# HGRN2 trunk on eight cores: two small per-chunk products moved to GpSimd, and ring slots given back two groups later

## The chip, the cores and the metric

One Trainium2 chip, all eight cores, one batch element per core; the cores do not talk to each other. The metric is the device time in microseconds of the slowest core. PE is TensorE, ACT ScalarE, DVE VectorE, POOL GpSimd and SP the sync engine.

## The reference, cut to what matters

Four pre-norm layers on a residual x of 2048 positions by 1024 channels. Layers 0 and 2 are an attention layer with a short convolution, layers 1 and 3 are HGRN2, a gated linear recurrence; each is followed by a SwiGLU. The change touches the HGRN2 layers alone. Cut to its core, one of them is, for each of 8 heads of 128 channels:

```python
q, f_logit, v, g_out = split(rms_norm(x) @ w_in, 4)
f = lb + (1 - lb) * sigmoid(f_logit);  k = 1 - f
for each chunk:                      # b = cumsum(log f) inside the chunk
    o     = (q * exp(b)) @ state + (masked, decayed q k^T) @ v
    k_dec = k * exp(b_last - b)      # the decayed keys
    state = exp(b_last)[:, None] * state + k_dec.T @ v
o = o * rsqrt(mean(o*o)) * head_norm * silu(g_out);  x += o @ w_out
```

## The kernel before, in words

Everything is kept transposed, channels on partitions. The residual `xT_sb` (f32) and the normed input `hT_sb` (bf16) stay in SBUF, scratch is one tensor `U`, and the eight PSUM banks are `ps`. Each engine works its instructions off in the order in which they are written; a small tracker adds the semaphore waits. Thus an instruction that waits holds up all that stands behind it on its engine.

**An HGRN2 layer.** `hgrn_layer` works on chunks of 128 positions, 16 to a head, in four quarters q of four chunks. The order is written out by hand as a list of slots: `slot(P, fl)` issues one projection item from a list (8 matmuls of 128x512 for f, g and q, L884, or 16 of 128x256 for v, L933), and then what `at[P]` holds. A head n takes slots P0 = 16n and after: four f items, four g items, four v items (none in the last head, n = 7), four q items. The projection items rotate over PSUM banks 0 to 2. `pump` puts the evacuation of an item behind the matmuls of the next item, so the matmuls of item k can start only when the evacuation of item k-3 is done. The evacuations are on ACT for f (L897, sigmoid), g (L904, silu) and v (L945, copy), and on DVE for q (L914).

**What the slots carry beside the projections.** For head n: slot P0+8 has the logs of f (`prep_ln`, L954, ACT), slots P0+9 and P0+10 the prefix sums of the two halves (`prep_scan`, L961, DVE) and `prep_mid` (L969 to L973, DVE), slots P0+11 and P0+12 the exponentials of the two halves (`prep_exp`, L991 and L992, ACT; `prep_gsc`, L980 to L986, the factors per chunk, in `gsc`). Slots P0+13 to P0+16 have `prep_k` (L997, DVE), the keys of quarter q. For each quarter q, with c0 = P0+4q:

- slot c0+14, `b_ke`: the keys of the quarter times the chunk's factor, 128x512 in bf16, into one buffer `KE0` (L1004, DVE).
- slot c0+16, `b_ta`: PE transposes these (L1018) and makes the scores inside the chunks (L1026, L1028).
- slot c0+17, `b_kd`: DVE copies the transposes out (L1037) and masks the scores (L1039).
- slot c0+18, `b_u`: PE multiplies them with v (L1051).
- slot c0+19, `b_w`: for each chunk DVE adds to the running f32 state (L1067, L1064 for the first), and ACT makes a scaled bf16 copy of it, 128x128, in one of eight buffers `SB` (L1072).
- slot c0+22, `b_pvi`: PE multiplies scores with v (L1082) and the bf16 state with q (L1085); ACT squares the result (L1090). Then `b_og` (L1096), the norm (`b_ss` L1101, `b_norm` L1106 and L1109) and `b_ot` (L1115).

As c0 moves by four, slots of the form 4k+2 hold `b_u` of a quarter, `b_pvi` of the one before and `b_ke` of the next, and slots of the form 4k+3 hold `b_w`. The last head is followed by 22 slots in which the output projection (`OutProj`, L421, with the residual add L426) runs along.

**The weights.** `WStream` streams all weights through `ring`, 19456 bytes a partition, in the order of use. `release` marks a slot free, and `_pump` at once issues the next load that fits; the loads stand in POOL's queue (L268), and each waits there until the matmuls that read the old contents of its place are done. One head needs 10240 bytes of ring: 2048 each for f, g and q, 4096 for v. In an HGRN2 layer POOL does nothing else but these loads and two loads of output weights into `U` (L454). The releases are in `proj_items` and `v_items`, in the slot of the item's last matmuls.

Of the kernel before, what the change touches and what calls it, by code (L numbers as in the profile page):

```python
# [8 lines left out]
AF = mybir.ActivationFunctionType  # L9
ALU = mybir.AluOpType  # L10
# [110 lines left out]
def flat_res(*items):  # L121
    out = []
    for it in items:
        if isinstance(it, Res):
            out.append(it)
        elif isinstance(it, Buf):
            out.extend(it.res)
        else:
            for x in it:
                out.extend(flat_res(x))  # L130
    return out

def build(layers, final, n_ab, n_c, n_ffn, comps=("mix", "ffn")):
    nc = bass.Bass("TRN2", target_bir_lowering=False)
    es = contextlib.ExitStack()
    T = Tracker()
# [23 lines left out]
    with es:  # L160
# [16 lines left out]
        ACT = Eng(nc, es, "act", nc.scalar)  # L177
        DVE = Eng(nc, es, "dve", nc.vector)
        POOL = Eng(nc, es, "pool", nc.gpsimd)
# [27 lines left out]
        def abuf(off, nbytes, dt=BF16, parts=128, shape=None):  # L207
            assert off % 4 == 0 and off + nbytes <= NUNITS * 4096
            ap = Uf[0:parts, off // 2:(off + nbytes) // 2]
            if dt == F32:  # L210
                ap = ap.bitcast(F32)
            if shape is not None:
                ap = ap.rearrange(shape[0], **shape[1])
            return Buf(ap, u_res[off // GRAN:(off + nbytes - 1) // GRAN + 1])
# [13 lines left out]
        class WStream:  # L228
            def __init__(self):
                self.plan = []  # L230
                self.i_issue = 0
                self.i_get = 0
                self.live = []
                self.head = 0
                self.slots = {}

            def _place(self, nbytes):
                nb = -(-nbytes // GRAN) * GRAN
                if not self.live:
                    return 0, nb  # L240
                tail = self.live[0][0]
                if self.head > tail:
                    if self.head + nb <= RING_BYTES:
                        return self.head, nb
                    if nb <= tail:
                        return 0, nb
                    return None
                if self.head + nb <= tail:
                    return self.head, nb
                return None  # L250
# [33 lines left out]
                    self._pump()  # L284
                return self.slots.pop(i)

            def release(self, bf):
                if T.plan:
                    return
                for e in self.live:  # L290
                    if e[2] == bf.widx:
                        e[3] = True
                while self.live and self.live[0][3]:
                    self.live.pop(0)
                self._pump()

        W = WStream()

# [535 lines left out]
        def hgrn_layer(gl, ci, rd, gnext):  # L834
# [7 lines left out]
            def quarter(base, q, n=1, dt=BF16):  # L842
                sz = 1024 if dt == BF16 else 2048
                return abuf(base + q * sz, n * sz, dt)
# [15 lines left out]
            def pump(fl):  # L860
                if fl:
                    mm, evac = fl.pop(0)
                    b = nbank[0] % 3
                    nbank[0] += 1
                    mm(b)
                    pend.append((evac, b))
                    if len(pend) > 1:
                        e, eb = pend.pop(0)
                        e(eb)
# [6 lines left out]
            def proj_items(key, src, h, evac):  # L876
                w = W.get((key, gl, h), src, NKC, 128)
                fl = []
                for q in range(4):
                    def mm(b, q=q):  # L880
                        def fn():
                            inst = None
                            for kc in range(NKC):
                                inst = nc.tensor.matmul(ps[:, b, :], lhsT=w.ap[:, kc, :],  # L884
                                                        rhs=hT[:, kc, q * 512:(q + 1) * 512],
                                                        start=(kc == 0), stop=(kc == NKC - 1))
                            return inst
                        T.op(PE, fn, reads=flat_res(w, h_res), writes=[bank[b]])
                        if q == 3:
                            W.release(w)  # L890
                    fl.append((mm, lambda b, q=q: evac(b, q)))
                return fl

# [25 lines left out]
            def v_items(pair, part, parts):  # L919
                n = 8 // parts  # L920
                w = W.get(("c_v", gl, pair, part), c_v_d[ci, pair], NKC, 256)
                fl = []
                for i in range(n):
                    t2 = part * n + i

                    def mm(b, t2=t2, i=i):
                        def fn():
                            inst = None
                            for k in range(2):
                                o = ps[:, b, :].rearrange("p (a k e) -> p a k e", a=2, k=2)[:, :, k, :]  # L930
                                tt = 2 * t2 + k
                                for kc in range(NKC):
                                    inst = nc.tensor.matmul(o, lhsT=hT[:, kc, tt * 128:(tt + 1) * 128],  # L933
                                                            rhs=w.ap[:, kc, :].rearrange("p (a e) -> p a e", a=2),
                                                            start=(kc == 0), stop=(kc == NKC - 1))
                            return inst
                        T.op(PE, fn, reads=flat_res(w, h_res), writes=[bank[b]])
                        if i == n - 1:
                            W.release(w)

                    def evac(b, t2=t2):
                        o = Uf[:, 2 * pair * 2048:(2 * pair + 2) * 2048].rearrange("p (a x) -> p a x", a=2)[
                            :, :, t2 * 256:(t2 + 1) * 256]
                        res = [r for a in range(2) for r in abuf((2 * pair + a) * 4096 + t2 * 512, 512).res]
                        T.op(ACT, lambda: nc.scalar.copy(out=o, in_=ps[:, b, :].rearrange("p (a x) -> p a x", a=2)),  # L945
                             reads=[bank[b]], writes=res)
                    fl.append((mm, evac))
                return fl
# [52 lines left out]
            def b_ke(h, q):  # L1001
                n = 4 if q < 3 else 3
                kt, ke = KT(q), quarter(KE0, 0)
                T.op(DVE, lambda: nc.vector.tensor_tensor(  # L1004
                    out=ke.ap[:, 0:n * 128].rearrange("p (a c) -> p a c", a=n),
                    in0=kt.ap[:, 0:n * 128].rearrange("p (a c) -> p a c", a=n),
                    in1=gsc[:, h % 2, 0, 4 * q:4 * q + n].rearrange("p (c o) -> p c o", o=1).broadcast_to([128, n, 128]),
                    op=ALU.mult),
                    reads=flat_res(kt, gsc_res[h % 2]), writes=ke.res)
# [46 lines left out]
            def b_w(h, q):  # L1056
                n = 4 if q < 3 else 3
                for i in range(n):
                    c = 4 * q + i
                    u = ps[:, 6, i * 128:(i + 1) * 128]  # L1060
                    sn, sp = Wb[c % 4], Wb[(c - 1) % 4]
                    gr = gsc_res[h % 2]
                    if c == 0:
                        T.op(DVE, lambda: nc.vector.tensor_copy(out=sn.ap, in_=u), reads=[bank[6]], writes=sn.res)  # L1064
                    else:
                        b12 = gsc[:, h % 2, 2, c - 1:c]
                        T.op(DVE, lambda: nc.vector.scalar_tensor_tensor(out=sn.ap, in0=sp.ap, scalar=b12, in1=u,  # L1067
                                                                         op0=ALU.mult, op1=ALU.add),
                             reads=flat_res(sp, gr, bank[6]), writes=sn.res)
                    b1 = gsc[:, h % 2, 1, c:c + 1]  # L1070
                    sbn = SB[(c + 1) % 8]
                    T.op(ACT, lambda: nc.scalar.activation(out=sbn.ap, in_=sn.ap, func=AF.Copy, scale=b1),  # L1072
                         reads=flat_res(sn, gr), writes=sbn.res)

            def b_pvi(h, q):
# [81 lines left out]
                    at[P0 + 13 + q].insert(0, (prep_k, (q,))) if P0 + 13 + q in at else put(P0 + 13 + q, prep_k, q)  # L1157

            def slot(P, fl):
                if fl:  # L1160
                    pump(fl)
                for fn, args in at.get(P, []):
                    fn(*args)
# [10 lines left out]
            for k in range(8):  # L1174
                slot(4 + k, v)
# [180 lines left out]
```

How the kernel before makes its waits and increments, by code:

```python
    def _wait(self, eng, reads, writes):  # L82
        deps = {}
        for r in reads:
            self._merge(deps, r.writers)
        for w in writes:
            self._merge(deps, w.writers)
            self._merge(deps, w.readers)
        for so, v in deps.items():
            if so is eng and eng.skip_self:
                continue
            if eng.waited.get(so, 0) >= v:
                continue
            eng.h.wait_ge(so.sem, v)
            eng.waited[so] = v
# [1 line left out]
    def op(self, eng, fn, reads=(), writes=()):  # L97
# [3 lines left out]
        inst = fn()  # L101
        eng.cnt += 1
        inst.then_inc(eng.sem, 1)
        for r in reads:
# [1136 lines left out]
        def body():  # L1241
            stages = []
            for (gl, mi, fi) in layers:
                if "mix" in comps:
                    stages.append((hgrn_layer if gl % 2 else fox_layer, gl, mi, C_GMIX + gl * 8))
                if "ffn" in comps:
                    stages.append((ffn, gl, fi, C_GFFN + gl * 8))
            gnext = [s[3] for s in stages[1:]] + [C_GFIN if final else None]
            rd = first_norm(stages[0][3])
            for k, ((fn, gl, i, _), gn) in enumerate(zip(stages, gnext)):
                rd = fn(gl, i, rd, gn)
                if k == 0:
                    T.dma(POOL, sem_cst, lambda: nc.gpsimd.dma_start(out=cst[:, K_SCAN:NCONST], in_=const_d[:, K_SCAN:NCONST]),
                          writes=[scan_res])
            rd.need(3)
            if not T.plan:
                nc.sync.wait_ge(sem_out.sem, sem_out.cnt)
```

## Time and profile before

| | us |
|---|---|
| median of 3 runs | 3595.34 |
| the three runs | 3595.34, 3595.16, 3924.01 |
| the profiled execution, its own time | 3592.3 |
| its span, slowest core (core 5) | 3591.3 |
| spans of all cores | 3582.7 to 3591.3 |

Busy share of core 5: PE 93%, DVE 40%, ACT 36%, POOL 4%. The two HGRN2 layers take about 925 to 1330 us and 2770 to 3180 us of the span. In a row of a timeline the first number is the start and the second the length in us; xN says how many instructions the row merges; what stands in brackets is the idle time of the engine before it and what ended it. "PEclk" is the clock granted to TensorE, 1.00 being 2.4 GHz and 0.50 being 1.2 GHz; in a stretch where it changed it is the mean.

### The profile page before, as it was taken

The page shows a single profiled execution, that of the slowest core. Times are in us where ns is not written, and L with a number is a line of the kernel's source. Part 1 is how long each engine was busy: PE and PEld are TensorE (multiplying, and loading weights), DVE is VectorE, ACT ScalarE, POOL GpSimd, SP SyncE. Part 2 cuts the span into 40 slices and gives each one's busy share as a digit, 9 for nine tenths or more (in the row PEclk, how much of TensorE's full clock was granted, in tenths as well). Part 3 has the DMA queues.
Part 4 walks back from the last instruction along what each step waited for, and adds up shares of the span by engine and source line. Part 5 has one row for each costly group of instructions (what it writes and reads, how often), then busy time and mean ns, then how long its engine had stood idle before and what let it go on. Part 6 is the DMA issues. An engine that isn't in the chain of part 4 may idle for free.

```text
span 3591.3 us, 47292 instructions; the slowest of 8 cores (3582.7 to 3591.3 us)
## 1 busy us (share of the span) xinstructions
PE 3344.1 (93%) x17264; PEld 1604.9 (45%) x17264; DVE 1447.6 (40%) x2159; ACT 1290.8 (36%) x2067; POOL 156.2 (4%) x256
## 2 busy tenths in 40 slices
PE   6999999999888889999989898999998888899998
PEld 2444344444454434444445443444444554344443
DVE  6443521113467672111374445111145667611215
ACT  3666511002477741101236564110135776411013
POOL 1000000000000000000020000000000000000000
PEclk9999999999999999999999999999999999999999
DMA  5111132121122113112100110312201221131212
GB/s 130 22 19 24 18 62 40 31 47 27 19 33 36 19 30 59 34 31 47 24 15 13 31 30 13 64 28 43 42 15 30 36 33 30 18 64 33 38 30 94
DMA packets 42289, 131.00 MB, mean 36 GB/s; under 512 B 4448, under 2 KB 4704, under 8 KB 42048
## 3 DMA queue, kind: packets, MB, share of 16 engines
q0 software_dynamic: 33120, 110.54, 17.9%
q1 hardware_dynamic: 8944, 17.44, 1.5%
q8 instruction: 144, 2.36, 0.3%
q14 instruction: 81, 0.66, 0.1%
HBM read 229.90 MB, written 8.59 MB: 66 GB/s over the span
## 4 chain that ended last, share of the span: by engine, by line
PE 86%; ACT 5%; DVE 4%; issue 3%; DMA 1%; ACTq 0%; DVEq 0%; SPq 0%; POOLq 0%; POOL 0%
PE ps L304 32%; PE ps L421 11%; PE ps L507 11%; PE ps L314 10%; PE ps L884 9%; PE ps L817 4%; PE ps L754 3%; PE ps L342 2%; PE ps L646 2%; PE ps L933 2%; DVE hT_sb L360 1%; DVE xT_sb L426 1%; ACT U L799 1%; DVE U L1067 1%; ACT U L954 1%
## 5 line engine op out<-in xcount | busy, mean ns | idle before, releaser
L304 PE MATMUL ps<-hT_sb,ring 128*128 128x512 bf16 x5248 | 1134.0, 379 | 6.7 <-ACT U L484 6.7
L304 PEld LDWEIGHTS ps<-hT_sb,ring 128*128 128x128 bf16 x5248 | 513.2, 98 | 626.8 <-issue 8.5
L484 ACT ACTIVATE U<-ps 128x2048 bf16<-128x2048 f32 x88 | 165.2, 1877 | 1371.4 <-PE ps L304 1371.3
L487 DVE TENSOR_TENSOR U<-U,ps 128x2048 bf16<-128x2048 bf16 x84 | 192.1, 2287 | 950.2 <-PE ps L304 923.0
L884 PE MATMUL ps<-hT_sb,ring 128*128 128x512 bf16 x1536 | 377.1, 399 | 74.4 <-ACT U L945 45.8
L314 PE MATMUL ps<-hT_sb,ring 128*128 128x512 bf16 (+1 forms) x1728 | 410.0, 385 | 25.2 <-DVE U L624 11.1
L507 PE MATMUL ps<-U,ring 128*128 128x512 bf16 x1792 | 387.4, 379 | 0.0
L799 ACT ACTIVATE U<-ps 128x512 bf16<-128x512 f32 (+3 forms) x640 | 303.3, 536 | 208.5 <-PE ps L758 122.1
L421 PE MATMUL ps<-U 128*128 128x512 bf16 x1536 | 372.5, 383 | 3.8 <-DMA U<-c_out 2.6
L426 DVE TENSOR_TENSOR xT_sb<-xT_sb,ps 128x512 f32<-128x512 f32 x320 | 218.4, 686 | 206.3 <-PE ps L421 187.2
L332 ACT ACTIVATE U<-xT_sb 128x512 bf16<-128x512 f32 x288 | 177.7, 628 | 287.1 <-DVE xT_sb L426 274.7
L507 PEld LDWEIGHTS ps<-U,ring 128*128 128x128 bf16 x1792 | 175.3, 98 | 211.5
L314 PEld LDWEIGHTS ps<-hT_sb,ring 128*128 128x128 bf16 (+1 forms) x1728 | 166.0, 98 | 228.3 <-issue 44.8
L884 PEld LDWEIGHTS ps<-hT_sb,ring 128*128 128x128 bf16 x1536 | 152.7, 102 | 257.0 <-issue 110.4
L817 PE MATMUL ps<-U 128*128 128x512 bf16 (+3 forms) x640 | 219.6, 347 | 34.2 <-ACT U L799 32.9
L421 PEld LDWEIGHTS ps<-U 128*128 128x128 bf16 x1536 | 150.2, 98 | 182.2 <-issue 8.1
L754 PE MATMUL ps<-U 70*128 70x512 bf16 (+3 forms) x640 | 220.7, 349 | 0.0
L512 DVE TENSOR_TENSOR xT_sb<-xT_sb,ps 128x2048 f32<-128x2048 f32 x32 | 73.2, 2287 | 313.6 <-PE ps L507 313.6
L360 DVE SCALAR_TENSOR_TENSOR hT_sb<-xT_sb,small_sb,U 128x512 bf16<-128x512 f32 x256 | 183.6, 746 | 37.4 <-ACT U L348 34.3
L342 PE MATMUL ps<-U,cst_sb 128*128 128x512 bf16 x288 | 115.4, 411 | 52.5 <-ACT U L332 36.6
L933 PE MATMUL ps<-ring,hT_sb 128*128 128x256 bf16 x1024 | 119.0, 273 | 20.4 <-ACT U L945 20.4
L1072 ACT ACTIVATE U<-U,gsc 128x128 bf16<-128x128 f32 x240 | 95.9, 402 | 113.2 <-DVE U L1067 91.5
(113 smaller groups left out, 2522.9 us busy)
## 6 DMA issues: line engine op xcount, KB each, us to landing
ring<-ffn_in POOLq DMA_DIRECT2D x88, 512.0 KB, 5.3
ring<-ffn_out POOLq DMA_DIRECT2D x16, 896.0 KB, 7.1
xT_sb<-xT SPq DMA_DIRECT2D x8, 1024.0 KB, 19.5
U<-ffn_out POOLq DMA_DIRECT2D x16, 512.0 KB, 12.1
yT<-xT_sb SPq DMA_DIRECT2D x16, 512.0 KB, 2.9
ring<-c_v POOLq DMA_DIRECT2D x14, 512.0 KB, 5.3
ring<-ab_qk POOLq DMA_DIRECT2D x8, 512.0 KB, 6.4
ring<-ab_cx POOLq DMA_DIRECT2D x8, 512.0 KB, 6.5
```

The source lines that it names most:

```text
L304: inst = nc.tensor.matmul(ps[0:m, banks[tt], :], lhsT=w.ap[:, kc, c0:c0 + m], rhs=hT[:, kc, tt * 512:(tt + 1) * 512], start=(kc == 0), sto ...
L314: inst = nc.tensor.matmul(ps[0:m, b, :], lhsT=w.ap[:, kc, c0:c0 + m], rhs=hT[:, kc, t * 512:(t + 1) * 512], start=(kc == 0), stop=(kc == N ...
L360: T.op(DVE, lambda: nc.vector.scalar_tensor_tensor(out=dst[:, c, sl], in0=xT[:, c, sl], scalar=small[:, self.gcol + c:self.gcol + c + 1], ...
L421: inst = nc.tensor.matmul(ps[:, b, :], lhsT=w.ap[:, self.jmap[j], cs], rhs=rr[j - j0].ap, start=(j == ja), stop=(j == jb - 1))
L426: T.op(DVE, lambda: nc.vector.tensor_tensor(out=xT[:, dc, sl], in0=xT[:, dc, sl], in1=ps[:, b, :], op=ALU.add), reads=[bank[b], x_res[dc][ ...
L487: T.op(DVE, lambda: nc.vector.tensor_tensor(out=v4(ubuf(jj, 1).ap), in0=v4(st.ap), in1=ps[:, 4:8, :], op=ALU.mult), reads=flat_res(st, ban ...
L507: inst = nc.tensor.matmul(ps[:, b0 + tt, :], lhsT=wo.ap[:, j, dcl * 128:(dcl + 1) * 128], rhs=a.ap[:, tt * 512:(tt + 1) * 512], start=(j = ...
L754: inst = nc.tensor.matmul(ps[:, sbk, off:512], lhsT=k_.ap[0:70, j * 128:(j + 1) * 128], rhs=q_.ap[0:70, qt * 512 + off:(qt + 1) * 512], st ...
L799: T.op(ACT, lambda: nc.scalar.activation(out=pt.ap[:, off:512], in_=ps[:, sbk, off:512], func=AF.Exp), reads=[bank[sbk]], writes=pt.res)
L817: T.op(PE, lambda: nc.tensor.matmul(ps[:, ob, off:512], lhsT=v.ap[:, j, vs], rhs=pt.ap[:, off:512], start=(j == 0), stop=(j == 4 * qt + 3) ...
L884: inst = nc.tensor.matmul(ps[:, b, :], lhsT=w.ap[:, kc, :], rhs=hT[:, kc, q * 512:(q + 1) * 512], start=(kc == 0), stop=(kc == NKC - 1))
L933: inst = nc.tensor.matmul(o, lhsT=hT[:, kc, tt * 128:(tt + 1) * 128], rhs=w.ap[:, kc, :].rearrange("p (a e) -> p a e", a=2), start=(kc == ...
```

## The change

It does three things.

- `b_ke` issues its product on POOL in place of DVE.
- In `b_w` the bf16 copy of the state is a `tensor_scalar` on POOL in place of an `activation` on ACT.
- In `proj_items` and `v_items` the ring slot is not released at once. It is put on a list with a count of two. `tick`, called at the start of every slot of an HGRN2 layer, counts down, and releases what has come to zero: the next load of the ring is issued at the start of the second slot after the one with the item's last matmuls.

```diff
+            def release(self, bf, late=False):
                 if T.plan:
+                    return
+                if late:
+                    self.late.append([2, bf])
                     return
...
+            def tick(self):
+                for e in self.late:
+                    e[0] -= 1
+                while self.late and self.late[0][0] <= 0:
+                    self.release(self.late.pop(0)[1])
...
                         if q == 3:
-                            W.release(w)
+                            W.release(w, True)
...
                         if i == n - 1:
-                            W.release(w)
+                            W.release(w, True)
...
                 kt, ke = KT(q), quarter(KE0, 0)
-                T.op(DVE, lambda: nc.vector.tensor_tensor(
+                T.op(POOL, lambda: nc.gpsimd.tensor_tensor(
...
                     sbn = SB[(c + 1) % 8]
-                    T.op(ACT, lambda: nc.scalar.activation(out=sbn.ap, in_=sn.ap, func=AF.Copy, scale=b1),
+                    T.op(POOL, lambda: nc.gpsimd.tensor_scalar(out=sbn.ap, in0=sn.ap, scalar1=b1, scalar2=None, op0=ALU.mult),
...
             def slot(P, fl):
+                W.tick()
                 if fl:
                     pump(fl)
```

ACT before, in slots P0+8 to P0+12 of a middle head. L954 is the logs, L945 the evacuations of v, L1106 and L1109 the norm, L1090 the square, L1072 the state copies, L991 and L992 the exponentials of the first half:

```order
L954 ACTIVATE U<-U,deriv_sb 128x1024 x2
L945 CAST U<-ps 128x2x256 x2
L1106 ACTIVATE U<-ps,deriv_sb 128x512
L1109 ACTIVATE U<-U 128x512
L1090 ACTIVATE U<-ps 128x512
L945 CAST U<-ps 128x2x256
L1072 ACTIVATE U<-U,gsc 128x128 x4
L991 ACTIVATE U<-U 128x1024
L992 ACTIVATE U<-U 128x1024
L945 CAST U<-ps 128x2x256
```

The same place of the changed kernel, where the lines stand 10 lower in the file (L955 is the old L945, L1001 the old L991):

```order
L964 ACTIVATE U<-U,deriv_sb 128x1024 x2
L955 CAST U<-ps 128x2x256 x2
L1116 ACTIVATE U<-ps,deriv_sb 128x512
L1119 ACTIVATE U<-U 128x512
L1100 ACTIVATE U<-ps 128x512
L955 CAST U<-ps 128x2x256
L1001 ACTIVATE U<-U 128x1024
L1002 ACTIVATE U<-U 128x1024
L955 CAST U<-ps 128x2x256
```

Four copies no longer stand between the third evacuation of v and the exponentials, behind which the fourth evacuation of v stands; all else keeps its order.

POOL before, over a little more than one middle head, is loads alone:

```order
L268 DMA ring<-c_g 128x1024
L268 DMA ring<-c_v 128x2048
L268 DMA ring<-c_q 128x1024
L268 DMA ring<-c_f 128x1024
L268 DMA ring<-c_g 128x1024
```

POOL of the changed kernel over one middle head (L1014 is `b_ke`, L1082 the state copies, L269 a ring load):

```order
L1014 TENSOR_TENSOR U<-U,gsc 128x512
L1082 TENSOR_SCALAR U<-U,gsc 128x128 x4
L269 DMA ring<-c_q 128x1024
L1014 TENSOR_TENSOR U<-U,gsc 128x512
L1082 TENSOR_SCALAR U<-U,gsc 128x128 x4
L269 DMA ring<-c_f 128x1024
L1014 TENSOR_TENSOR U<-U,gsc 128x384
L1082 TENSOR_SCALAR U<-U,gsc 128x128 x4
L269 DMA ring<-c_g 128x1024
L1014 TENSOR_TENSOR U<-U,gsc 128x512
L1082 TENSOR_SCALAR U<-U,gsc 128x128 x3
```

Each group of copies (slot 4k+3) is followed by the ring load that was given back late (slot 4k+5), and then by the next quarter's decayed keys (slot 4k+6).

## Rows read from the trace of the kernel before

**Rows 1.** The page, busy time, share of span, instructions of each engine.

```profile
PE 3344.1 (93%) x17264; PEld 1604.9 (45%) x17264; DVE 1447.6 (40%) x2159; ACT 1290.8 (36%) x2067; POOL 156.2 (4%) x256
```

**Rows 2.** Waits of PE, 925 to 1330: total us, times, longest.

```profile
PE ps L884 <- ACT U L945: 23.1, 6, 4.1
PE ps L933 <- ACT U L945: 10.1, 9, 1.5
...
PE ps L884 <- ACT U L904: 5.8, 1, 5.8
```

**Rows 3.** Waits of PE, 2770 to 3180.

```profile
PE ps L884 <- ACT U L945: 22.7, 6, 3.8
```

**Rows 4.** Busy time by stretch, one middle head from one long wait to the next.

```profile
core 5: us, PE busy (x) PEld busy (x) DVE busy (x) ACT busy (x) POOL busy (x), PEclk, DMA share, GB/s
...
1044.87:1085.56 40.69, 35.75 (x258) 21.15 (x259) 28.20 (x54) 29.61 (x50) 2.11 (x4) 0.96 0.21 33
```

**Rows 5.** Timeline of PE, 1044 to 1090.

```profile
1065.74 1.89 PE L884 MATMUL ps<-hT_sb,ring 128*128 128x512 bf16 x8
...
1075.58 1.91 PE L933 MATMUL ps<-ring,hT_sb 128*128 128x256 bf16 x16 [1.15 <-ACT U L945]
...
1085.56 2.83 PE L884 MATMUL ps<-hT_sb,ring 128*128 128x512 bf16 x8 [3.79 <-ACT U L945]
1088.18 0.53 PE L1051 MATMUL ps<-U 128*128 128x128 bf16 x3
```

**Rows 6.** Timeline of ACT, 1044 to 1090.

```profile
1067.80 1.70 ACT L1072 ACTIVATE U<-U,gsc 128x128 bf16<-128x128 f32 x4 [0.71 <-DVE U L1067]
1069.40 0.58 ACT L904 ACTIVATE U<-ps 128x512 bf16<-128x512 f32 x1
...
1072.61 2.36 ACT L954 ACTIVATE U<-U,deriv_sb 128x1024 f32<-128x1024 f32 x2
...
1077.61 0.58 ACT L945 CAST U<-ps 128x512 bf16<-128x512 f32 x1
1081.09 1.76 ACT L1072 ACTIVATE U<-U,gsc 128x128 bf16<-128x128 f32 x4 [2.90 <-DVE U L1067]
1082.75 1.04 ACT L991 ACTIVATE U<-U 128x1024 f32<-128x1024 f32 x1
...
1084.85 0.57 ACT L945 CAST U<-ps 128x512 bf16<-128x512 f32 x1
```

**Rows 7.** Timeline of DVE, 1044 to 1090.

```profile
1073.94 2.29 DVE L961 TENSOR_TENSOR_SCAN U<-cst_sb,U 128x1024 f32<-128x1024 bf16 x1 [0.38 <-ACT U L954]
1076.14 0.53 DVE L1004 TENSOR_TENSOR U<-U,gsc 128x384 bf16<-128x384 bf16 x1
...
1080.65 1.70 DVE L1067 SCALAR_TENSOR_TENSOR U<-U,gsc,ps 128x128 f32<-128x128 f32 x4
...
1085.66 0.35 DVE L1037 COPY U<-ps 128x384 bf16<-128x384 bf16 x1
```

**Rows 8.** Busy time by stretch, the 3.8 us behind the long wait.

```profile
1085.56:1089.35 3.79, 3.79 (x19) 2.16 (x20) 3.57 (x7) 3.20 (x5) 0.00 (x0) 0.60 0.00 0
```

**Rows 9.** Groups of instructions, 925 to 1330: busy us, mean ns, idle before.

```profile
L1072 ACT ACTIVATE U<-U,gsc 128x128 bf16<-128x128 f32 x120 | 47.9, 402 | 57.1 <-DVE U L1067 46.1 <-DVE U L1064 6.1 <-ACT U L1072 0.4
...
L1004 DVE TENSOR_TENSOR U<-U,gsc 128x512 bf16<-128x512 bf16 (+1 forms) x32 | 20.7, 646 | 0.0
```

**Rows 10.** Groups of POOL by shape, whole span.

```profile
L611 POOL MEMSET U<- 6x2048 bf16 x8 | 14.4, 1797 | 1.2 <-POOL U L610 0.5 <-DVE U L701 0.2
...
L134 POOL MEMSET const-float32-0.0<- 128x1 f32 x1 | 0.1, 103 | 0.5 <-issue 0.5
```

**Rows 11.** Timeline of POOL, 1085 to 1127, first ring load.

```profile
1091.99 0.53 POOL L268 DMA_DIRECT2D ring<-c_v  x1 [13.44 <-PE ps L884]
```

**Rows 12.** Timeline of the last head, PE and DVE, 1200 to 1330.

```profile
1249.57 3.57 PE L884 MATMUL ps<-hT_sb,ring 128*128 128x512 bf16 x8 [5.81 <-ACT U L904]
1252.94 0.52 PE L1051 MATMUL ps<-U 128*128 128x128 bf16 x3
...
1248.24 0.35 DVE L1037 COPY U<-ps 128x384 bf16<-128x384 bf16 x1
```

More of the change, by code:

```diff
@@ L235, in __init__ @@
                 self.slots = {}
+                self.late = []
             def _place(self, nbytes):
@@ L285, in get @@
                 return self.slots.pop(i)
-            def release(self, bf):
+            def release(self, bf, late=False):
                 if T.plan:
+                    return
+                if late:
+                    self.late.append([2, bf])
                     return
```

## The prediction, made before the changed kernel was timed

> **What bounds the kernel now.** The page comes first: PE is busy 93% of the span and every other engine 40% or less [rows 1]. So a change on ACT, DVE or POOL pays only where PE waits for them, and the next view is the waits of PE in the two HGRN2 layers. There the reader is to see one pattern. The projection matmuls L884 wait for the evacuation L945 six times a layer, some 3.8 us each, 23.1 and 22.7 us in all [rows 2, 3]. The v items L933 wait for the same line for 10.1 us, and one wait of 5.8 us is for L904 [rows 2]. No PE wait of the stage is for a ring load. In the view by stretches a middle head takes 40.69 us, with ACT busy 29.6 and DVE 28.2 of them [rows 4]: neither is full, so what counts is the order in which they do things.
>
> The timelines of one head say why PE waits. The q item at 1085.56 waits 3.79 us for its bank [rows 5], which the evacuation at 1084.85 frees. ACT gets to it late: after the v evacuation at 1077.61 it idles 2.90 us for DVE's state updates L1067, makes four state copies (1081.09), then the two exponentials (from 1082.75), and only then evacuates [rows 6]. The matmuls of that v item had been done since 1077.5 (1075.58 + 1.91) [rows 5]. The wait has a second price: in the 3.79 us behind it the granted clock is 0.60, a mixture of 1.2 and 2.4 GHz, and the eight matmuls take 2.83 us where eight at full clock take 8 x 0.216 = 1.73 (the row of 1.89 for eight counts one tail) [rows 5, 8].
>
> **The change part by part.** *State copies off ACT.* 120 instructions of 402 ns a layer go, and with them 57.1 us in which ACT stood before them [rows 9]. I replay one head.
>
> Slot P0+8: the copies at 1067.80 go. The last evacuation of g (1069.40) needs only the matmuls started at 1065.74, done at 1067.5, so it and all behind it come 1.8 us earlier. That holds for the logs (1072.61 to 1070.8) and for the scan that waits for them (1073.94 to 1072.1) [rows 5 to 7]. The 1.15 us wait of the v item at 1075.58 goes [rows 5].
>
> Slots P0+11 and P0+12: ACT, after the third v evacuation (1077.61, now about 1076.1), runs the exponentials, 2.1 us, and evacuates at 1078.8, done at 1079.4. PE has nothing left before its third q item at 1085.56 - 3.79 - 1.15 = 1080.6. The bank is free before that: the long wait goes as such.
>
> What is late next? The item is followed by `b_u` (L1051, at 1088.18), which needs DVE's copy L1037 (1085.66, 0.35 long) [rows 5, 7]. From the scan to L1037, DVE works almost without a gap, so L1037 moves only by what its chain moves: 1.8 us from the earlier scan and 0.5 from the L1004 that leaves DVE (1076.14) [rows 7], to 1083.4, done at 1083.7. With 0.1 us of hand-over `b_u` starts at 1083.9. PE is done with the item at 1082.3 and so waits 1.6 us for DVE in place of 3.79 for ACT. `b_u` is 4.3 us earlier. The granted clock: PE's 1.15 us wait before 1077.5 left it at full (the next eight matmuls start to start at 0.216), the 3.79 did not; I take it that 1.6 leaves it. The matmuls from `b_u` on to 1089.35 then take some 0.4 us less, and those just behind another 0.4. In all 5.1 us of the 40.69.
>
> *Decayed keys off DVE.* 32 instructions of 646 ns a layer, 20.7 us [rows 9]. Outside the stretch above DVE's gaps hide them; the 0.5 is counted. From L1037 on, DVE has four q evacuations, keys and updates to do, which end the bank wait of a later item; one more L1004 fewer there keeps it just ahead of PE.
>
> *The same work on POOL.* POOL had 2.11 us of work in a head [rows 4] and gets 15 copies and 4 products. No row shows a POOL instruction that reads a tile. A copy costs no less than 0.1 us (the 128x1 memset, 103 ns) and, at most, the longest POOL row, 1.8 (1797 ns) [rows 10]. I take 0.45, near ACT's 402 ns. For a product the ends are the same; I take 1.3, twice DVE's 646 ns. That is 15 x 0.45 + 4 x 1.3 + 2.1 = 14 us a head of some 36: no bound. Nor is it late. The first update ends at 1080.65 + 0.4 - 2.3 = 1078.8, PE reads the third copy just behind `b_u`, at 1084: 5.2 us for three copies. The product has two slots, over 4 us.
>
> What POOL does to DVE's own steps has no row either. It is between 0 and one POOL instruction, 1.8 us, in the stretch up to L1037; I take 0.5, the size of one copy. So 5.1 - 0.5 = 4.6 us a head.
>
> The Trainium skill has a rule that speaks against this change: "SBUF — State Buffer", section "Who interferes with whom", says a DVE instruction with two SBUF inputs and a GpSimd instruction that reads SBUF shut each other out for a whole instruction. By it the L961, L973, L997 and L1115 of that stretch could each meet a POOL instruction; this trace has no reading POOL instruction and shows nothing on it. What it would make of the time is the second rival below.
>
> *The late ring slots.* A load waits in POOL's queue for the matmuls that free its place (13.44 us before the one at 1091.99) [rows 11]. Behind it would now stand copies; two slots later those matmuls are done when POOL arrives, so the load holds POOL 0.53 us and no longer. The loads come two slots, some 4.5 us, later; the ring of 19456 bytes holds 1.9 heads of 10240, so each still lands tens of us before use. I count nothing, from 0 up to the 4.5 us once a layer if a load were just in time.
>
> *The last head and the tail.* There PE waits 5.81 us for L904 and starts `b_u` at 1252.94, while L1037 stands at 1248.24 [rows 12]. By the same 2.3 us L1037 ends at 1246.3, `b_u` at 1246.4: 6.5 us less, 6.0 after the 0.5, and 0.5 for the clock. In the tail three L1004 and 16 copies leave a crowded DVE and ACT; 1 us.
>
> **The sum.** A layer: 6 x 4.6 + 6.5 + 1 = 35.1 us. Two: 70.2. The second layer's waits are the same size [rows 2, 3]. The profiled execution took 3592.3 us, so 3522.1; the median of the runs is 3.0 us above it, so 3525.
>
> **Rivals.** *All of the wait goes.* If PE did not wait for DVE either, a head would lose 3.79 + 1.15 + 1.1 + 0.7 = 6.7 us: 2 x (6 x 6.7 + 7 + 2) = 98, so 3497. For it: DVE is busy only 28.2 of 40.7. Against it: between the scan and L1037 it has no gap left.
>
> *DVE is held by POOL, or POOL's instructions are long.* If each of three two-input steps of the stretch loses one copy or product, 1.5 to 2 us more, or if the 2 to 3 us wait that is left still brings the clock to 1.2 GHz for the item behind (1.1 us), a head gains 2 us: 2 x (12 + 5) = 34, so 3561. The page named above is the case for it. Against it: POOL's rows for small work are short.
>
> *The copies were not what held ACT.* Then the time stays at 3595. Against it stand 2.90 us of ACT idle in front of L1072 [rows 6].
>
> *Slower: POOL becomes the bound.* With copies of c us and products of 1.8, a head costs POOL 15c + 7.2 + 2.1. PE starts to wait for the third copy from c = 5.2 / 3 = 1.7, and the head is longer than 40.69 from c = 2.1. At c = 2.5 it is 46.8, 6.1 us more in 14 heads: 3680. For it: nothing in the trace bounds a reading POOL instruction. Against it: even 6x2048 elements take 1.8 [rows 10].
>
> **How the numbers follow.** Forecast 0.55, all of the wait gone 0.12, held DVE 0.22, nothing 0.05, slower 0.06. The forecast's own range, with the coupling between 0 and 1 us, is 3510 to 3540. The range that should hold the time 8 times in 10 reaches into the first two rivals: 3502 to 3572. A measurement of this kernel tells about 2%, 72 us, from no change, that is 3523. A little under half of the forecast's share lies below it (0.26), with the first rival and a little for gains in places not counted, 0.41. Slower by over 2% is the last rival but for its mild part, 0.05. The rest, 0.54, is within.
>
> **What would show it.** Right: in the HGRN2 layers the waits of L884 for the v evacuation are gone or below 1 us; a wait of 1 to 2.5 us of L1051 for DVE's copy stands in their place; a middle head takes 35.5 to 37 us; the granted clock stays at full in all middle heads; POOL copies of 0.3 to 0.6 us. Wrong: PE waiting for POOL in L1018 or L1085; DVE steps L1115, L997 or L961 longer than their 0.75, 0.69 and 2.3 us; a middle head still at 39 us or more; PE waiting for a ring load.

## The result, and the profile after

The changed kernel took **3569.5 us** (median of three runs, 3565.4 to 3569.6; a fourth, with one die at a much lower clock, took 3808.7) against 3595.3 before: ratio **0.9925, 95% interval 0.9896 to 0.9953**, 26 us less. In each of the three runs two or four cores of one die had a mean granted clock of about 0.974, and the last of them ended 20 to 25 us after the slowest of the rest, whose spans are 3533 to 3545 us. The first experiment, the same kernel again, gave one run without such cores, 3545.2 us: that is what the change does by itself.

The page of the profiled execution, against [rows 1]:

```profile
span 3568.5 us, 47925 instructions; the slowest of 8 cores (3534.2 to 3568.5 us)
PE 3355.3 (94%) x17264; PEld 1608.3 (45%) x17264; DVE 1428.5 (40%) x2095; ACT 1203.3 (34%) x1827; POOL 383.7 (11%) x560
```

Lines stand 10 lower in the file than before: L884 is L894, L933 L943, L945 L955, L961 L971, L1037 L1047, L1051 L1061, L1067 L1077, L1072 L1082, L1115 L1125; L1004 is L1014.

First these cores. Busy time by stretch, in a part of the first attention layer that the change does not touch, for core 4 (one of them) and core 0, in this order. The columns are those of [rows 4]: engines busy, then the granted clock, DMA share, GB/s.

```profile
core 4 of [0, 1, 2, 3, 4, 5, 6, 7], span 3568.5 us
74.60:186.00 111.40, 105.78 (x510) 52.18 (x507) 44.79 (x91) 52.50 (x104) 10.27 (x9) 0.81 0.14 24
192.80:234.30 41.50, 40.82 (x233) 23.91 (x231) 14.41 (x41) 21.34 (x42) 0.00 (x0) 0.81 0.01 2
```

```profile
74.60:186.00 111.40, 103.39 (x612) 57.95 (x621) 51.18 (x110) 61.74 (x125) 10.62 (x10) 0.98 0.14 24
192.80:234.30 41.50, 39.73 (x215) 19.88 (x218) 19.62 (x35) 25.50 (x52) 0.00 (x0) 1.00 0.01 2
```

In the first stretch core 0 executes 612 matmuls and core 4 510. No instruction of the edit runs here, and the kernel before has such runs too, as the experiments show. The rows below are of core 0, and where they are of core 4 they are from a layer in which it stood at full clock.

The Trainium skill, "TensorE: Matmul & The Clock Gate", Part 1, tells of a peak-current limit that puts a whole die at 13/16 of the clock once three of its cores run dense matmuls, and holds it while they do. The level agrees (0.81 is 13/16), the rest does not: PE is busy 94% of core 4's span, and here one die stood at it for two stretches only, 153 us together. Nor is it always a whole die: in the trace of the third experiment cores 0, 1, 4 and 5 stood at 0.81 for 156 to 160 us, and the other two cores of each die did not.

The waits of PE in the first HGRN2 layer, core 0, against [rows 2]:

```profile
PE ps L1061 <- DVE U L1047: 15.4, 7, 2.7
PE ps L894 <- ACT U L914: 4.5, 1, 4.5
PE ps L943 <- ACT U L955: 4.4, 4, 1.5
```

The six waits of 3.8 us for the v evacuation are gone, and half of those of the v items. In their place stands the wait of `b_u` for DVE's copy of the last quarter, seven times, up to 2.7 us. One of them in the timeline of PE, and the same place a head later:

```profile
1075.33 0.33 PE L1061 MATMUL ps<-U 128*128 128x128 bf16 x3 [2.36 <-DVE U L1047]
...
1075.94 3.62 PE L894 MATMUL ps<-hT_sb,ring 128*128 128x512 bf16 x16
...
1111.62 0.33 PE L1061 MATMUL ps<-U 128*128 128x128 bf16 x3 [2.36 <-DVE U L1047]
...
1112.24 5.28 PE L894 MATMUL ps<-hT_sb,ring 128*128 128x512 bf16 x16
```

The same wait stands before both, and the 16 matmuls behind it take 3.62 us the one time and 5.28 the other. The stretches say why. Each but the last row runs from one start of `b_u` to the next; the last is what follows the wait at 1111.62.

```profile
1039.00:1075.30 36.30, 33.50 (x253) 20.31 (x257) 27.63 (x50) 24.19 (x35) 16.61 (x24) 1.00 0.23 37
1075.30:1111.60 36.30, 33.50 (x253) 20.36 (x258) 27.62 (x50) 24.19 (x35) 16.61 (x24) 1.00 0.24 37
1111.60:1149.60 38.00, 35.20 (x254) 20.87 (x259) 27.24 (x50) 24.21 (x35) 17.17 (x25) 0.96 0.21 35
1149.60:1187.90 38.30, 35.16 (x254) 21.09 (x258) 26.30 (x50) 24.16 (x35) 15.53 (x22) 0.95 0.18 29
...
1111.60:1116.50 4.90, 4.88 (x23) 2.25 (x24) 4.84 (x8) 1.34 (x2) 0.92 (x1) 0.65 0.27 48
```

A head takes 36.3 us where the clock stays, and 38.0 to 38.3 where it falls to 1.2 GHz behind the wait. By the starts of `b_u` on all eight cores, in both layers of this trace and of that of the first experiment, it fell behind 86 of the 128 waits of 2.36 to 2.70 us in the middle heads, and behind none of the 32 of 1.77 us with which the first of them begins. By the same starts of `b_u` (last quarter) a head of before takes 40.4 to 41.1 on core 0.

POOL's work, grouped, and one head of its timeline with DVE's chain beside it (core 0; the groups are core 4's):

```profile
L1082 POOL TENSOR_SCALAR U<-U,gsc 128x128 bf16<-128x128 f32 x120 | 81.1, 684 | 161.6 <-DVE U L1077 135.1 <-DVE U L1074 24.8 <-POOL U L1082 1.7
L1014 POOL TENSOR_TENSOR U<-U,gsc 128x512 bf16<-128x512 bf16 (+1 forms) x32 | 32.0, 1001 | 10.6 <-DVE U L1047 6.8 <-DVE U L1007 2.4 <-PE ps L1028 1.0
```

```profile
1061.79 0.84 POOL L1014 TENSOR_TENSOR U<-U,gsc 128x384 bf16<-128x384 bf16 x1
1070.16 1.19 POOL L1082 TENSOR_SCALAR U<-U,gsc 128x128 bf16<-128x128 f32 x2 [7.53 <-DVE U L1077]
1071.52 2.17 POOL L1082 TENSOR_SCALAR U<-U,gsc 128x128 bf16<-128x128 f32 x2 [0.17 <-DVE U L1077]
...
1075.19 1.03 POOL L1014 TENSOR_TENSOR U<-U,gsc 128x512 bf16<-128x512 bf16 x1 [0.95 <-DVE U L1047]
```

```profile
1061.99 1.19 DVE L1125 SCALAR_TENSOR_TENSOR U<-U,small_sb 128x512 bf16<-128x512 f32 x1 [0.45 <-ACT U L1119]
1063.13 2.29 DVE L971 TENSOR_TENSOR_SCAN U<-cst_sb,U 128x1024 f32<-128x1024 bf16 x1
...
1069.59 0.34 DVE L1077 SCALAR_TENSOR_TENSOR U<-U,gsc,ps 128x128 f32<-128x128 f32 x1
1070.10 0.35 DVE L1077 SCALAR_TENSOR_TENSOR U<-U,gsc,ps 128x128 f32<-128x128 f32 x1 [0.17 <-DVE U L1077]
...
1071.41 0.75 DVE L1125 SCALAR_TENSOR_TENSOR U<-U,small_sb 128x512 bf16<-128x512 f32 x1
...
1074.84 0.35 DVE L1047 COPY U<-ps 128x384 bf16<-128x384 bf16 x1
1075.10 0.68 DVE L1049 TENSOR_TENSOR U<-ps,cst_sb 128x512 bf16<-128x512 f32 x1
1075.70 1.08 DVE L1125 SCALAR_TENSOR_TENSOR U<-U,small_sb 128x512 bf16<-128x512 f32 x1
```

Two things are to be seen. L1125 takes 0.75 us alone, and 1.19 and 1.08 beside the products at 1061.79 and 1075.19; POOL's pair of copies takes 1.19 beside DVE's updates, which read SBUF with one input, and 2.17 beside L1125 and what follows. And from the scan to the copy L1047 it is 1074.84 - 1063.13 = 11.71 us, against 1085.66 - 1073.94 = 11.72 before [rows 7], although L1004 has left this chain.

### The profile page after: what moved, and what is told of

Read it like the earlier page. It is cut to its first block, busy times and chain, and to the rows that moved or that the text cites. A ratio compares the mean times of both kernels' runs of the same rounds, so it can differ in the third digit from the quotient of the medians.

```text
span 3568.5 us, 47925 instructions; the slowest of 8 cores (3534.2 to 3568.5 us)
## 1 busy us (share of the span) xinstructions
PE 3355.3 (94%) x17264; PEld 1608.3 (45%) x17264; DVE 1428.5 (40%) x2095; ACT 1203.3 (34%) x1827; POOL 383.7 (11%) x560
## 3 DMA queue, kind: packets, MB, share of 16 engines
q8 instruction: 144, 2.36, 0.3%
## 4 chain that ended last, share of the span: by engine, by line
PE 86%; DVE 5%; issue 4%; ACT 3%; DMA 1%; POOL 0%; DVEq 0%; ACTq 0%; SPq 0%; POOLq 0%
PE ps L314 32%; PE ps L431 11%; PE ps L517 11%; PE ps L324 10%; PE ps L894 8%; PE ps L827 4%; PE ps L764 3%; PE ps L943 2%; PE ps L656 2%; PE ps L352 2%; DVE hT_sb L370 1%; DVE xT_sb L436 1%; DVE U L1077 1%; DMA xT_sb<-xT 1%; ACT U L809 1%
## 5 line engine op out<-in xcount | busy, mean ns | idle before, releaser
L324 PE MATMUL ps<-hT_sb,ring 128*128 128x512 bf16 (+1 forms) x1728 | 419.9, 392 | 27.8 <-DVE U L634 12.5
L894 PE MATMUL ps<-hT_sb,ring 128*128 128x512 bf16 x1536 | 366.9, 393 | 26.3 <-DVE hT_sb L370 17.1
L894 PEld LDWEIGHTS ps<-hT_sb,ring 128*128 128x128 bf16 x1536 | 151.7, 101 | 203.9 <-issue 54.4
L370 DVE SCALAR_TENSOR_TENSOR hT_sb<-xT_sb,small_sb,U 128x512 bf16<-128x512 f32 x256 | 183.6, 746 | 39.0 <-ACT U L358 35.9
L1082 POOL TENSOR_SCALAR U<-U,gsc 128x128 bf16<-128x128 f32 x240 | 162.1, 684 | 324.0 <-DVE U L1077 269.5
L269 POOL DMA_DIRECT2D ring<-ffn_in x88 | 47.1, 536 | 1287.7 <-PE ps L314 687.1
```

Source lines behind the costliest of these rows:

```text
L324: inst = nc.tensor.matmul(ps[0:m, b, :], lhsT=w.ap[:, kc, c0:c0 + m], rhs=hT[:, kc, t * 512:(t + 1) * 512], start=(kc == 0), stop=(kc == N ...
L370: T.op(DVE, lambda: nc.vector.scalar_tensor_tensor(out=dst[:, c, sl], in0=xT[:, c, sl], scalar=small[:, self.gcol + c:self.gcol + c + 1], ...
L894: inst = nc.tensor.matmul(ps[:, b, :], lhsT=w.ap[:, kc, :], rhs=hT[:, kc, q * 512:(q + 1) * 512], start=(kc == 0), stop=(kc == NKC - 1))
```

## The experiments

Three chips were used; ratios are to runs of before on the same chip. The times are those of runs without cores at 0.81 in the first attention layer; where there were others, they stand behind. Before took 3595.5 and 3597.0 on the chip of the first four kernels (others 3612 to 3633), 3594.5 to 3595.0 on that of the next four, 3593.6 to 3596.1 on that of the last two.

**The change itself again.**

> The changed kernel once more, as it is. In the first measurement the four cores of one die were 25 us slower than the others, and all of it lay in the first attention layer, in which no instruction is changed, where their granted clock was 0.812 for 153 us. If that is a state of the chip and no work of the change, undisturbed cores take 3534 to 3545 us again and a clean run about 3545, 1.4% less than before. If the change itself causes it, every run has a die near 3565.

Measured: 3545.2, others 3564.2 to 3569.8; ratio 0.9861 (0.9828 to 0.9894). Without such cores the change is worth **50 us, 1.4%**. That is one run, but the eight spans of its trace, 3531.3 to 3544.1, lie where the cores at full clock of all other runs of this kernel do. The 20 to 25 us between it and the first measurement are in both kernels: before has its 3616 beside 3596.

**Copies alone**: the state copies on POOL, the keys back on DVE, ring places given back at once.

```
-  T.op(POOL, lambda: nc.gpsimd.tensor_tensor(
+  T.op(DVE, lambda: nc.vector.tensor_tensor(
-  W.release(w, True)
+  W.release(w)
```

> Only the state copies move to GpSimd; keys stay on DVE, ring slots are released at once. Main theory (the copies held ACT, DVE's chain is now the bound): the wait for the v evacuation is gone, the wait of the state matmul for DVE's copy is 0.5 us longer than with the keys moved (2.9 in place of 2.36), so 10 us above the changed kernel, 3555. Rival (moving the keys is what pays): near 3590.

**Keys alone**: the keys on POOL, the state copies on ACT, released at once.

```
-  T.op(POOL, lambda: nc.gpsimd.tensor_scalar(out=sbn.ap, in0=sn.ap, scalar1=b1, scalar2=None, op0=ALU.mult),
+  T.op(ACT, lambda: nc.scalar.activation(out=sbn.ap, in_=sn.ap, func=AF.Copy, scale=b1),
-  W.release(w, True)
+  W.release(w)
```

> Only the decayed keys move to GpSimd; copies stay on ACT, ring slots are released at once. Main theory: ACT still stands before its copies, so the long wait stays at 3.3 to 3.8 us and the time is 3583 to 3592. Rival (DVE's load is what holds everything): 3550 to 3570.

**Not late**: copies and keys on POOL, `W.release(w)` in place of `W.release(w, True)`.

> The changed kernel with ring slots released at once. If the late release matters, the load now stands in GpSimd's queue ahead of the copies of the same slot and waits there for the projection matmuls of that slot, 1 to 2 us; the copies have some 5 us, so I expect 0 to 5 us more than the changed kernel. A rival in which POOL is short of time gives 15 us or more.

Measured, in that order: 3547.7 to 3549.1, another 3571.1 (ratio 0.9836, 0.9795 to 0.9877); 3586.1 and 3588.1, others 3604 to 3634 (0.9984, 0.9948 to 1.0021); 3552.8, others 3571 and 3576 (0.9871, 0.9824 to 0.9917). The waits of PE with the copies alone, then with the keys alone:

```profile
PE ps L1061 <- DVE U L1047: 16.5, 8, 2.5
```

```profile
PE ps L894 <- ACT U L955: 21.2, 6, 3.5
PE ps L894 <- ACT U L914: 7.7, 1, 7.7
```

The copies are 48 of the 50 us and do by themselves what the whole change does to the pattern of waits. The wait is 2.53 us, not the 2.9 expected. The trace without the late release, with the keys moved as well, has 2.52: taking the keys off DVE does nothing for this wait, though a head at full clock takes 36.4 us there and 36.8 with the copies alone.

The keys alone leave the pattern of before and gain 9 us or so. Their ratio can't tell that from nothing, but the traces can: a middle head takes 39.9 us on average on each of the eight cores in both layers, where before has 40.4 to 40.6.

On top of the copies the keys cost 4 us without the late release and gain 3 with it. The late release, which I had counted at nothing, is worth 8 us by one run, and 3 to 4 by the dies at full clock in the others, whose slowest cores end at 3545 to 3549 where those of the changed kernel end at 3542 to 3545. A part of it is in the rows. Without it the key product on POOL reaches into DVE's scan, which takes 2.45 us in place of 2.29 (core 2, at full clock in this layer), and the wait of `b_u` is 2.52 in place of 2.36:

```profile
1060.39 1.32 POOL L1014 TENSOR_TENSOR U<-U,gsc 128x384 bf16<-128x384 bf16 x1
1061.41 2.45 DVE L971 TENSOR_TENSOR_SCAN U<-cst_sb,U 128x1024 f32<-128x1024 bf16 x1 [0.38 <-ACT U L964]
```

That is 0.16 us a head, some 2 us in all; the rest is open.

**The copies stay on ACT, but later.** If what mattered is that they stood ahead of the evacuation, it should help to issue them behind it. Nothing is on POOL, and the copies, taken out of `b_w` into a `b_wc` of their own, come a slot after the updates.

```
     put(c0 + 19, b_w, n, q)
+    put(c0 + 20, b_wc, n, q)
```

> The kernel before, with nothing on GpSimd; only the state copies are issued one slot later on ACT (slot c0+20), behind the exponentials and the v evacuation instead of ahead of them. Main theory in its strong form (it was the order on ACT and not its load): the long wait goes just as in the changed kernel, a state matmul waits 2.5 to 3.5 us for DVE's copy, the time is 3545 to 3560. Rival (ACT's load must go to another engine): 3580 or more.

Measured: 3563.6 to 3567.6, ratio 0.992 (0.9901 to 0.994), between the 3545 to 3560 of the main theory and the 3580 of the rival. The long waits for the v evacuation are gone and `b_u` waits for DVE, as in the changed kernel (line numbers of before):

```profile
PE ps L1051 <- DVE U L1037: 14.3, 7, 2.6
PE ps L933 <- ACT U L945: 8.9, 9, 1.5
```

So some 28 us, of the 50 of the change, come from the order on ACT alone, without a single instruction leaving it. Taking the work off ACT gives the rest: where the clock stays the head is 38.4 us here, against 36.3, and the v items' waits of 8.9 stay.

**The copy L1047 of the last quarter earlier.** It is cut out of its item `b_kd` as `b_kdc` and issued a slot sooner, so `b_u` does not wait for it.

```
+    put(c0 + 16 if q == 3 and n < 7 else c0 + 17, b_kdc, n, q)
     put(c0 + 17, b_kd, n, q)
```

> The changed kernel with one DVE instruction moved: the copy of the transposed keys (old L1037) of a head's last quarter is issued in slot P0+12, ahead of the midpoint work of the next head, instead of behind it. If DVE's chain up to this copy is the whole bound now, the 2.36 us wait falls to 1 us or less (a bank wait for the first q evacuation takes its place), the clock no longer falls to 1.2 GHz behind it, a head takes 34.5 to 35.5 us, and the time is 3515 to 3528. Rival (POOL or the rest of DVE holds PE as well): within 5 us of 3545.

Measured: 3535.3 to 3536.9, ratio 0.9838 (0.9818 to 0.9857): 9 us below the changed kernel's 3545.2 of another chip, not the 17 or more expected. `b_u` no longer waits, but the time it waited is there again, in two pieces, at the next q evacuation (timeline of PE, core 3):

```profile
1075.08 1.89 PE L894 MATMUL ps<-hT_sb,ring 128*128 128x512 bf16 x8 [1.13 <-DVE U L924]
1078.20 1.89 PE L894 MATMUL ps<-hT_sb,ring 128*128 128x512 bf16 x8 [1.23 <-DVE U L924]
```

1.13 + 1.23 = 2.36 us, to the hundredth what `b_u` waited. What it gained is the clock. Three of the stretches from one `b_u` to the next, on core 7:

```profile
998.10:1034.10 36.00, 34.22 (x259) 20.33 (x257) 27.32 (x50) 23.30 (x33) 16.35 (x24) 1.00 0.22 38
...
1107.20:1143.70 36.50, 34.13 (x259) 20.32 (x258) 27.82 (x50) 24.04 (x35) 16.05 (x24) 1.00 0.23 37
1143.70:1180.30 36.60, 34.23 (x258) 20.22 (x257) 26.65 (x49) 23.79 (x35) 15.51 (x23) 1.00 0.18 30
```

No middle head is left at 38; on all eight cores and in both layers they take 35.9 to 36.7, and the granted clock of each is 1.00. The five of a layer take 182.2 us in both layers, where the trace of the first experiment has 185.1 and, as a mean of the cores, 186.2: 7 of the 9 us. So a wait of 2.36 us in one piece was followed by the lower clock in two of three heads, and the same wait in two pieces in none of 64.

**No copies at all, and the copies twice.** The first leaves out the `tensor_scalar` of L1082, the second makes each of them twice.

> The changed kernel with the state copies left out altogether: the state matmuls read buffers that hold zeros, so the contribution of earlier chunks is missing. It bounds what GpSimd's copies still cost (locking DVE out, the extra semaphore wait in DVE's updates). My account gives them 0.26 us for four slower updates and 0.1 to 0.3 us for a longer copy of the chunk factors: the wait falls from 2.36 to about 2.0 us, 12 heads times 0.4 and perhaps fewer clock drops, 3525 to 3540. Rival (the copies cost nothing): 3545.

> The changed kernel with every state copy on GpSimd made twice. A copy is 0.68 us from start to start, so three pairs take 4.1 us where I counted 5.2 us of slack. Main theory: POOL is not the bound, PE does not wait for it; DVE is held a little more often, 0 to 10 us more than 3545. Rival (POOL is already close to the path): 3580 or more, with waits of the state matmuls for POOL.

Measured: without the copies 3531.1 to 3537.0 (ratio 0.9832, 0.981 to 0.9855), twice 3572.2 to 3573.6 (0.9939, 0.9917 to 0.9962). Without them `b_u` still waits for DVE, 2.05 us in place of 2.36:

```profile
PE ps L1061 <- DVE U L1047: 13.1, 7, 2.1
```

So the copies cost the changed kernel 8 to 14 us, against its one run of 3545.2 on another chip, and the wait for DVE is for the most part not their doing. Both are as expected. The 0.31 are DVE's own steps, which without the copies are as before: the four updates run in 1.70 us in place of 1.90, and one small copy of the factors (L981) takes 0.17 in place of 0.26. Behind 30 of 64 waits of 2.05 us the clock still fell. Made twice, the copies cost 27 to 28 us more, where I had expected at most 10 and the rival had 35:

```profile
PE ps L1093 <- POOL U L1083: 10.5, 8, 3.4
PE ps L1061 <- DVE U L1047: 9.5, 8, 1.8
...
PE ps L1028 <- POOL U L1014: 6.3, 5, 1.3
```

PE waits for POOL itself, the state matmuls for the copies (L1083) and the transposes for the keys. The timelines of POOL and DVE (core 3) show a pair of copies and a key product stretched beside DVE's two scans:

```profile
1065.65 3.51 POOL L1083 TENSOR_SCALAR U<-U,gsc 128x128 bf16<-128x128 f32 x2 [0.17 <-POOL U L1083]
1069.33 1.12 POOL L1083 TENSOR_SCALAR U<-U,gsc 128x128 bf16<-128x128 f32 x1 [0.17 <-POOL U L1083]
...
1071.04 2.09 POOL L1014 TENSOR_TENSOR U<-U,gsc 128x384 bf16<-128x384 bf16 x1
```

```profile
1066.46 2.29 DVE L971 TENSOR_TENSOR_SCAN U<-cst_sb,U 128x1024 f32<-128x1024 bf16 x1 [0.38 <-ACT U L964]
...
1070.16 2.35 DVE L971 TENSOR_TENSOR_SCAN U<-cst_sb,U 128x1024 f32<-128x1024 bf16 x1 [0.17 <-DVE U L983]
```

**Two more orders of DVE's work**, on top of the early copy. The waiting evacuation L924 stands behind L1125 (now L1127), which the key product stretches to 1.34 us, and behind two small factor instructions. The first run moves L1127 back behind the updates, the second also the factors.

```
-    put(ln + 1, b_ot, n, q)
+    put(c0 + 27 if q == 1 and n < 7 else ln + 1, b_ot, n, q)
```

```
-    put(P0 + 12 - d, prep_gsc, n)
+    put(P0 + 13 if n else P0 + 12 - d, prep_gsc, n)
```

> The version with the scaled copy L1037 of the last quarter moved ahead, and with the o rows of the first piece (the DVE instruction that stood in slot 13 and that the key product on GpSimd stretched to 1.34 us) moved behind the w products. Theory (TensorE waits at L924 for the DVE because that stretched instruction stands before the queue-rows copy): the second of the two waits of a head, 1.23 us, goes, and 12 heads x 1.2 = 14 us leave: 3518 to 3526 against 3536. Rival (the DVE's total work in the stretch sets the end, its order does not): within 4 us of 3536, and the wait comes back at another copy.

> The run above with the two small instructions that prepare the decay factors moved one slot back behind the copy that TensorE waits for. Theory: the first wait shrinks by those two instructions and their semaphore waits, some 0.4 us a head, 3 to 6 us less than the run above. Rival (the matmuls of the new head's first piece wait for something other than the DVE): the same as the run above within 2 us.

Measured: 3532.7 to 3536.2 (ratio 0.983, 0.9811 to 0.985) and 3537.3 to 3539.5 (0.9842, 0.9823 to 0.9861). The first fell to its rival: within 4 us of 3536, and the wait is back at another copy. The second met neither expectation: it is 4 to 5 us slower than the first, on the same chip, and its middle heads take 36.5 to 36.9 us against 36.0 to 36.7. With L1127 moved the 1.23 us wait goes, and comes back further on (PE, core 3, first run; L1063 is `b_u` here, L1046 the copy it waits for):

```profile
1075.53 3.74 PE L894 MATMUL ps<-hT_sb,ring 128*128 128x512 bf16 x16 [1.13 <-DVE U L924]
...
1082.49 1.89 PE L894 MATMUL ps<-hT_sb,ring 128*128 128x512 bf16 x8 [0.61 <-DVE U L924]
1084.82 0.38 PE L1063 MATMUL ps<-U 128*128 128x128 bf16 x4 [0.45 <-DVE U L1046]
```

1.13 + 0.61 + 0.45 = 2.19 us. The new holder is a meeting again, a DVE instruction with two inputs beside POOL's key product at 1082.73, 2.08 us where the same line takes 0.68 elsewhere in the head:

```profile
1078.42 0.68 DVE L1007 SCALAR_TENSOR_TENSOR U<-U 128x512 bf16<-128x512 f32 x1
...
1082.26 2.08 DVE L1007 SCALAR_TENSOR_TENSOR U<-U 128x512 bf16<-128x512 f32 x1
```

The version with the early copy, at 3536, and the one with L1127 moved, at 3534, are both faster than the two kernels of this case, by 58 and 62 us against before on their chips and by some 9 and 12 against the change's 3545.2.

## Why the prediction was right or wrong

The forecast was 3525 us, 70 less than before. Measured were 26 less, and 50 in the run without cores at 0.81. The range (3502 to 3572) holds both, the size does not. Of the 44 us between 70 and 26, 24 are those cores, and 20 are steps of the working. Point by point:

- **The copies held ACT, and their removal ends the long wait.** Right, and shown from three sides: the 3.79 and 1.15 us waits are gone, the copies alone do it, and so does a mere later place for them on ACT. The rival that they were not the cause falls.
- **`b_u` then waits for DVE's copy, 1.6 us.** Right in place; the size is the step that failed, and the clock hung on it. The wait was 2.36. My own 0.5 for POOL's coupling, taken for this very stretch, would have made it 2.1, but the clock was judged at 1.6. Of the 0.8 between them 0.5 is the term "0.5 from the L1004": from scan to copy the chain is 11.71 us, as before. L1004 was 0.53 us long, but the steps behind it came only 0.25 earlier by its going, and 0.30 went back to POOL's copies (0.20 in the four updates, 0.10 in L981). Another 0.2 is the scan, which against PE's work came 1.6 us earlier and not 1.8, as did the evacuation of g ahead of it. L1125, stretched to 1.19 in front of the scan, cost nothing: the scan starts 1.14 us after the start of L1125 before (L1115) and after.
- **"I take it that 1.6 leaves it."** At 1.6 it would have: behind 1.77 us the clock stayed in all 32 cases. Behind 2.36 us it fell to 1.2 GHz in two of three middle heads, 1.7 to 2.0 us each (5.28 against 3.62 us for 16 matmuls), and the sum has nothing for that. My own second rival named it ("if the 2 to 3 us wait that is left still brings the clock to 1.2 GHz"), at 0.22. The early copy shows the wait to be the cause: the same 2.36 us in two pieces, and the 38 us heads are gone.
- **A head of 4.6 us less.** Where the clock stays it is 4.1 (40.4 to 36.3). That is near; of the 0.5 taken for POOL's coupling 0.3 was there.
- **The sum of a layer.** On core 0 the first layer lost 26.0 us where I had 35.1. The five middle intervals gave 202.8 - 185.1 = 17.7 where 5 x 4.6 = 23.0 stood, 3.6 of the gap being two heads at 38.0 and 38.3; the last head 42.7 to 37.0, 5.7 against 6.5; the tail lost 0.9 where I had gained 1; the first head gave the rest, 3.5. In the second layer four of the five middle heads stood at 37.8 to 38.3, and their intervals gave 202.0 - 188.3 = 13.7. So the 20 us between 70 and 50 are the clock in six heads of that core, some 11, and terms each a little too large.
- **POOL.** Copies taken at 0.45 us took 0.68 (0.60 alone), products taken at 1.3 took 1.00. PE never waits for POOL, and the slower rival falls; but with the copies twice it does, so it was nearer than the "5.2 us for three copies" made it.
- **The late release counted at nothing** is worth 3 to 8 us.
- **DVE held by POOL (second rival).** The mechanism is there in the rows, L1125 at 1.08 to 1.19 for 0.75, but not its price of 1.5 to 2 us a head: without any copies the wait is only 0.3 us shorter. The Trainium skill, "SBUF — State Buffer", section "Who interferes with whom", has the rule, and these rows agree with it. That its 3561 is nearer to the measured 3569.5 than the forecast is luck: the 24 us of the die are not in it.
- **All of the wait goes (first rival).** It did not even with the copies out (2.05 us).

The other 24 us of the miss are the cores at 0.81 in the first attention layer. The sum has no term for them, and the rows cannot show what brings them about.

What stays open: where most of the late release's gain comes from, and what shortens DVE's chain as a whole, since with the early copy 2.36 us of wait are left a head, and 2.19 with L1127 moved too.

## What to carry to other kernels

When a wait for a helper engine is long, first try the order: here 28 of 50 us came from issuing the same copies one slot later on the same engine. When you work out what wait remains, ask of it too whether it brings the clock down, at a length a little over your estimate; where it cannot be removed, cut it in two. And before you reorder an engine for a few tenths, add up its chain between what releases it and what PE needs: if that is the bound, the wait only moves.

## What the runs showed of the hardware

- A 128x128 copy with a scale, f32 to bf16, takes GpSimd 0.60 us and ScalarE 0.40; a 128x512 bf16 product takes GpSimd 1.05 and VectorE 0.68 (means of 24).
- VectorE's scan shuts out a reading GpSimd instruction for its whole length: a pair of copies took 3.51 us beside a scan of 2.29, and 1.19 without. A scan begun beside a key product of GpSimd took 2.45.
- Four updates on VectorE that each wait for a GpSimd copy too start every 0.52 us, where those of before, and those of the kernel without copies, ran as a block of four in 1.70 (0.45 each). In the first quarter of a head the fourth has no new copy to wait for, and there it starts 0.45 after the third.
- 2.36 to 2.70 us of idle TensorE in one piece was followed by the granted clock of 1.2 GHz in 86 of 128 cases, 2.05 us in 30 of 64, 1.77 us in none of 32; 1.13 to 1.30 and 1.23 with eight matmuls between in none of 64. All are middle heads of both layers, on all eight cores.
